# A chunked RWKV-7 / GLA encoder step: the chunk inverse in four 32x32 tiles per head pair, the decay states added by VectorE, the last chunk iteration written out

## The reference, cut to what matters

```python
def step(s, inp):                     # GLA, one chunk of 64 tokens
    ...
    o = einsum('bhts,bhsv->bhtv', scores, vc) + einsum('bhtk,bhkv->bhtv', q_e, s)
    s_new = s * exp(last)[..., None] + einsum('bhsk,bhsv->bhkv', kc * exp(last - cum), vc)

def step(s, inp):                     # RWKV-7, one token
    rt, wt, kt, vt, at, bt = inp
    sa = einsum('bhvk,bhk->bhv', s, at)
    s = s * wt[:, :, None, :] + sa[..., None] * bt[:, :, None, :] + vt[..., None] * kt[:, :, None, :]
    y = einsum('bhvk,bhk->bhv', s, rt)
...
mu = mean(y, -1); var = mean(square(y - mu), -1)          # per head of 64
y = (y - mu) * rsqrt(var + RWKV_GN_EPS) * ln_w + ln_b
y = (y + bonus) * g
out = einsum('blc,cd->bld', concatenate([o_gla, y], -1), w_out[l])
```

## Time and profile before

| | us |
|---|---|
| median of the runs | 1740.63 (1739.42 to 1741.90, three runs) |
| the profiled execution | 1739.74, its span 1737.80 |
| chunk stage and first output pair, layer 0 | 209.80 to 411.04 of the span |
| the same in layer 1 | 1060.50 to 1260.90 |

### The profile page before, as it was taken

How to read it: one execution, slowest core, us unless ns; L and a number is a source line. 1 busy time by engine, 2 the same in 40 slices (tenths; PEclk the granted TensorE clock), 3 DMA queues, 4 the chain that set the end, 5 groups by cost and what they waited for, 6 DMA issues and landing times.

```text
span 1737.8 us, 42296 instructions
## 1 busy us (share of the span) xinstructions
PE 1691.0 (97%) x19069; PEld 1634.8 (94%) x19069; DVE 905.7 (52%) x1368; ACT 665.8 (38%) x1013; POOL 570.9 (33%) x303
## 2 busy tenths in 40 slices
PE   7999999988999999999999999999799999999997
PEld 7999999968999999999999999999699999999997
DVE  4669534344566504666546873343356662166643
ACT  5444344553433212333343534544434332133323
POOL 5443301113344433344333432011133443333431
PEclk9999999999999999999999999999899999999998
DMA  5223200001222322223322221000022223222331
GB/s 146 67 68 85 80 10 4 4 3 55 86 84 81 102 75 74 86 85 95 83 74 73 74 84 46 9 4 4 7 86 85 86 80 98 66 86 86 90 94 55
DMA packets 218869, 115.51 MB, mean 66 GB/s; under 512 B 9332, under 2 KB 216450, under 8 KB 218690
## 3 DMA queue, kind: packets, MB, share of 16 engines
q1 hardware_dynamic: 218610, 112.79, 22.6%
q10 hardware_dynamic: 80, 0.02, 0.0%
HBM read 109.27 MB, written 3.53 MB: 65 GB/s over the span
## 4 chain that ended last, share of the span: by engine, by line
PE 95%; ACT 2%; DVE 1%; POOL 1%; DMA 0%; issue 0%; SPq 0%; ACTq 0%; DVEq 0%; POOLq 0%
PE ps L583 37%; PE ps L584 36%; PE ps L800 2%; PE ps L804 2%; PE ps L762 2%; PE ps L796 2%; PE ps L775 1%; PE ps L588 1%; PE ps L923 1%; PE ps L906 1%; PE ps L839 1%; PE ps L866 1%; PE ps L966 1%; PE ps L698 1%; PE ps L975 1%; PE ps L847 1%
## 5 line engine op out<-in xcount | busy, mean ns | idle before, releaser
L508 POOL TENSOR_TENSOR wlo<-raw,whi 128x1024 fp32r<-128x1024 f32 (+1 forms) x188 | 508.6, 2705 | 804.5 <-ACT whi L1120 804.4
L1120 ACT ACTIVATE whi<-raw 128x1024 fp32r<-128x1024 f32 (+1 forms) x188 | 209.5, 1114 | 651.7 <-PE ps L584 651.7
L583 PE MATMUL ps<-xh,whi 128*128 128x288 f32 x1120 | 332.8, 297 | 4.1 <-DVE xl L1498 4.1
L584 PE MATMUL ps<-xh,whi 128*128 128x288 f32 x1120 | 331.2, 296 | 0.0
L583 PE MATMUL ps<-xl,whi 128*128 128x288 f32 x1120 | 330.3, 295 | 0.0
L584 PE MATMUL ps<-xl,whi 128*128 128x288 f32 x1120 | 329.1, 294 | 0.0
L583 PE MATMUL ps<-xh,wlo 128*128 128x288 f32 x1120 | 328.9, 294 | 0.0
L584 PE MATMUL ps<-xh,wlo 128*128 128x288 f32 x1120 | 328.6, 293 | 0.0
L583 PEld LDWEIGHTS ps<-xh,whi 128*128 128x128 f32 x1120 | 210.6, 188 | 6.2 <-issue 4.5
L584 PEld LDWEIGHTS ps<-xh,whi 128*128 128x128 f32 x1120 | 210.6, 188 | 0.2
L583 PEld LDWEIGHTS ps<-xh,wlo 128*128 128x128 f32 x1120 | 210.6, 188 | 0.0
(11 more groups left out here) (278 smaller groups left out, 3314.0 us busy)
## 6 DMA issues: line engine op xcount, KB each, us to landing
raw<-in_ffn_w_up SPq DMA_DIRECT2D x88, 512.0 KB, 3.8
raw<-in_w_in SPq DMA_DIRECT2D x52, 512.0 KB, 3.7
raw<-in_ffn_w_down SPq DMA_DIRECT2D x32, 704.0 KB, 4.5
raw<-in_w_out SPq DMA_DIRECT2D x16, 512.0 KB, 3.6
xin<-in_x_prompt SPq DMA_DIRECT2D x4, 512.0 KB, 6.5
out<-xin SPq DMA_DIRECT2D x8, 256.0 KB, 2.9
out<-RW SPq DMA_DIRECT2D x16, 64.0 KB, 2.2
g<-in_rwkv_g SPq DMA_DIRECT2D x2, 256.0 KB, 2.9
```

Of the source, the lines that this page charges most:

```text
L508: e.tensor_tensor(wlo[s][:, 0:width], raw[s][:, 0:width], whi[s][:, 0:width].bitcast(F32), ALU.subtract).then_inc(w_lo[s], 1)
L583: e.matmul(acc(out)[:, 0], lhsT, rhs[:, 0:HT], start=start, stop=stop)
L584: return e.matmul(acc(out)[:, 1], lhsT, rhs[:, HT:TOK], start=start, stop=stop)
L1120: e.activation(whi[s][:, 0:width], raw[s][:, 0:width], ACT.Copy).then_inc(w_hi[s], 1)
```

## The change

**Inverse in 32x32 tiles.** `DET` and `Tf` become 32 wide: of each pair of heads the four diagonal 32x32 blocks stand under one another on the 128 partitions. A generator `blocks()` yields the four; each product of `level` is issued four times on tiles of 32 rows by 32 columns instead of twice on 64 by 64. `gram` computes the blocks of E and of its transpose by itself on tiles of 64 rows by 32 columns, `mask_inverse` is one DVE operation in place of two, and `solve_z1` and `solve_u` multiply by `Tf` in four 32x32 tiles with 64 columns moving. `copy_powers`, `add_power` and POOL's `start_inverse` handle half the columns.

**Old states on VectorE.** The products with the identity (L878, L941) are gone. `new_state` and `new_gla_state` first add the PSUM sum to `St` or `Sg`, then multiply by the decay: two DVE operations in place of one.

**Last iteration written out.** The loop now runs to i = 7. There, group 3's RWKV statistics and group 4's GLA statistics are done (tables `O_AT`, `Y_AT`), the final GLA product is DVE's (`o_last`) instead of POOL's. Behind the loop chunk 8 is solved with work put between its steps; the last group's RWKV statistics are split by chunk: chunk 7's between the solve steps, chunk 8's behind `outputs`; DVE does the bias and gate work of groups 3 and 4 that POOL did, with the gate multiplied in ahead of the statistic. Of the first output pair, 42 of 48 products of the GLA half now stand behind the last statistic and ahead of the RWKV half.

```diff
                 def level(j, X, k):
...
                     for q in range(2):
-                        for hp in range(2):
-                            h = slice(64 * hp, 64 * hp + 64)
-                            if k < 4:
-                                mm = e.matmul(powers[h, q, 0], d[h, X, q, 2], d[h, X, q, 0], start=True, stop=True)
...
+                        if k < 4:
+                            for h, b, half in blocks():
+                                mm = e.matmul(powers[b, q, 0], d[b, X, q, 2], d[b, X, q, 0], start=True, stop=True)
+                        if k < 5:
+                            for h, b, half in blocks():
+                                mm = e.matmul(powers[b, q, 1], d[b, X, q, 0], d[b, X, q, 2], start=True, stop=True)
+                        if k > 1:
+                            for h, b, half in blocks():
+                                mm = e.matmul(product[b, q], d[b, X, q, 2], d[b, X, q, 1], start=True, stop=True)
                     mm.then_inc(pe_f, 1)
...
+                def blocks():
+
+                    for c in range(4):
+                        yield slice(64 * (c // 2), 64 * (c // 2) + 64), slice(B * c, B * c + B), c % 2
...
                     for p, X, q, o in pairs(ys[:, 256:512]):
                         for h in HEADS:
                             e.matmul(o[h], tok[i % 2][h, X, 1, q, :], tok[i % 2][h, X, 2, q, :], start=True, stop=False)
-                        if i != 1:
-                            for h in HEADS:
-                                e.matmul(o[h], ident2[h, :], St[h, p, :], start=False, stop=False)
...
                 def new_state(i):
                     step(pe_b, PE_B, i, "S")
-                    e.tensor_tensor(St[:, :, :], pair3(ys[:, 256:512]),
-                                    Plast[:, :, i:i + 1].broadcast_to([P, NP, C]), ALU.mult).then_inc(dv_b, 1)
+                    new = pair3(ys[:, 256:512])
+                    if i != 1:
+                        e.tensor_tensor(St[:, :, :], St[:, :, :], new, ALU.add).then_inc(dv_b, 1)
+                        step(dv_b, DV_B, i, "Sa")
+                        new = St[:, :, :]
+                    e.tensor_tensor(St[:, :, :], new,
+                                    Plast[:, :, i:i + 1].broadcast_to([P, NP, C]), ALU.mult).then_inc(dv_b, 2 if i == 1 else 1)
...
+                solve_z(LAST)
+                back(ac_b, AC_B, LAST - 1, "Y")
+                glas(dv_g, DV_G, LAST, "Sg")
+                chunk_mean(7, gb[:, 0:256], R[:, 0:4, seventh])
+                solve_z1(LAST)
+                solve_z2(LAST)
+                solve_u(LAST)
+                ending(ac_e, AC_E, "s7")
+                chunk_mean(7, gb[:, 256:512], squares[:, :, 0:C])
+                outputs(LAST)
+                back(ac_b, AC_B, LAST, "Y")
+                pe.wait_ge(ac_o, nth(AC_O, (l + 1) * len(GROUPS) - 1, "oln"))
+                chunk_mean(8, pb[:, 0:256], R[:, 0:4, eighth])
+                out_part(0, range(0, 1))
+                ending(ac_e, AC_E, "s8")
+                chunk_mean(8, pb[:, 256:512], squares[:, :, C:2 * C])
+                back(dv_b, DV_B, LAST, "St")
+                turn_state(St, zb)
+                out_part(0, range(1, 4))
+                out_part(1, range(0, 4))
+                out_part(0, range(4, 8))
+                out_part(1, range(4, 8))
```

More of the change, by code:

```diff
@@ L32 @@
 C = 64
+B = 32
 HT = TOK // 2
@@ L199, in program @@
         tok = [cut([P, 2, 3, 2, C]) for _ in range(2)]
-        DET = [cut([P, 2, 2, 3, C]) for _ in range(2)]
-        Tf = [cut([P, NP, C]) for _ in range(2)]
+        DET = [cut([P, 2, 2, 3, B]) for _ in range(2)]
+        Tf = [cut([P, NP, B]) for _ in range(2)]
         Z, Z1, W, U = (cut([P, NP, C]) for _ in range(4))
@@ L731, in _, with turn_state @@
                         wide(PS[3], g2[:, p * P:(p + 1) * P], R[:, 13]).then_inc(pre_pe, 1)
-                def turn_state(src):
+                def turn_state(src, out):
                     for p in range(NP):
@@ L837, in solve_z1 @@
                     for p, X, q, o in pairs(zb[:, 256:512]):
-                        for h in HEADS:
-                            mm = e.matmul(o[h], Tf[i % 2][h, p, :], Z[h, p, :], start=True, stop=True)
+                        for h, b, half in blocks():
+                            mm = e.matmul(o[b], Tf[i % 2][b, p, :], Z[b, p, :], start=True, stop=True)
                     mm.then_inc(pe_b, 1)
@@ L853, in solve_u @@
                     for p, X, q, o in pairs(zb[:, 256:512]):
-                        for h in HEADS:
-                            mm = e.matmul(o[h], Tf[i % 2][h, p, :], W[h, p, :], start=True, stop=True)
+                        for h, b, half in blocks():
+                            mm = e.matmul(o[b], Tf[i % 2][b, p, :], W[b, p, :], start=True, stop=True)
                     mm.then_inc(pe_b, 1)
@@ L979, in _ @@
                 dve("ke1")
-                for i in range(-1, NCH):
+                for i in range(-1, LAST):
                     j = i + 1
-                    post = i // 2 if i >= 0 and i % 2 == 0 else None
+                    po_, py = O_AT.get(i), Y_AT.get(i)
                     if i == 0:
                         pe.wait_ge(states_loaded, (l + 1) * 64)
-                        turn_state(Sraw)
+                        turn_state(Sraw, pb)
                     if i == 1:
                         back(dv_b, DV_B, 0, "St")
-                        turn_state(St)
+                        turn_state(St, pb)
@@ L1025, in _ @@
-                    if post is not None and post > 0:
-                        post_squares_y(post - 1)
-                    if j < NCH:
-                        gla_out(j)
-                        level(j, 0, 4)
-                        level(j, 1, 4)
-                        gla_state(j)
-                        level(j, 0, 5)
-                        level(j, 1, 5)
-                last = len(GROUPS) - 1
-                def out_part(s, half):
-                    if half == 0:
+                    level(j, 0, 2)
@@ new lines, in _ @@
+                    level(j, 1, 2)
+                    gla_tokens(j)
+                    level(j, 0, 3)
+                    level(j, 1, 3)
+                    if py is not None and i < LAST - 1:
+                        post_squares_y(py)
+                    gla_out(j)
+                    level(j, 0, 4)
+                    level(j, 1, 4)
+                    if i == LAST - 1:
+                        post_squares_o(po_)
+                    gla_state(j)
+                    level(j, 0, 5)
@@ L1039, in out_part @@
+                    level(j, 1, 5)
+                def out_part(s, kts):
+                    if 0 in kts:
                         pe.wait_ge(w_lo[s], turn(s, l, PAIRS["out"]) + 1)
                         pe.wait_ge(mo_lo, (l + 1) * len(GROUPS))
-                    else:
+                    if 4 in kts:
                         pe.wait_ge(my_lo, (l + 1) * len(GROUPS))
-                    for kt in range(4 * half, 4 * half + 4):
+                    for kt in kts:
                         mm = passes(s, mh, ml, kt, KT)
-                    if half:
+                    if KT - 1 in kts:
@@ L1046, in out_part @@
                         mm.then_inc(tile_done[s], 1)
[L1048 to L1056 removed]
+                seventh, eighth = slice((LAST - 1) * C, LAST * C), slice(LAST * C, TOK)
@@ L1905, in _ @@
-                    if post is not None:
-                        scale_o(post)
-                        if post > 0:
-                            scale_y(post - 1)
-                    if i >= 1 and i % 2 == 1:
+                    for k in (2, 3, 4):
+                        add_power(j, 0, k)
+                        add_power(j, 1, k)
+                    if i == LAST - 1:
+                        mixed_o(i // 2)
+                        mixed_y(i // 2 - 1)
+                    new_gla_state(j)
@@ new lines, in _ @@
+                    add_power(j, 0, 5)
+                    add_power(j, 1, 5)
+                    if po_ is not None:
+                        scale_o(po_)
+                    if i == LAST - 1:
+                        dv.wait_ge(silu_done, (l + 1) * NP)
+                        dv.wait_ge(dv_o, (l + 1) * len(GROUPS))
+                        cc = group(po_)[1]
+                        e.tensor_tensor(G[:, 4:8, cc], G[:, 4:8, cc], G[:, 8:12, cc], ALU.mult).then_inc(o_last, 1)
+                    elif py is not None:
+                        scale_y(py)
@@ L1910, in _ @@
+                    if i >= 1 and i % 2 == 1 and i < LAST - 1:
                         mixed_o(i // 2)
```

379 lines of the change are left out of this document (209 added, 170 removed).

## The result

| | before | changed |
|---|---|---|
| median, us | 1740.9 | 1792.1 (1786.3 to 1793.4) |
| ratio | 1 | 1.029 (95% interval 1.027 to 1.031) |
| span of the profiled execution | 1737.8 | 1784.3 |
| records of PE | 19069 | 23301 |

I had forecast 1706 us, faster, with a range up to 1754. The time is outside it, and the change made the kernel slower instead of faster. The profiled execution is the fastest of the four of the changed kernel, 5.7 us under their median.

A forecast was written before the change was run, and what follows sets the result against it. PE's queue was taken as the bound, busy 97% of the span. Loop -53.6 + 36.8 + 4 = -12.8 us and endings -21.6 us sum to -34.4 us, so 1706 us; range 1668 to 1754.

The forecast's parts named there:

- Part 1: Products replaced on PE: 132.2 us removed, 78.6 us added with small records at 8.25 ns, a gain of 53.6 us.
- Part 2: Changes of tile shape on PE: 250 more at 0.147 us each cost 36.8 us, lower bound nothing.
- Part 4: Waits in the loop: PE reaches z1 earlier but ACT's copy of Z does not, 4 us back.
- Rival 1: Changing between 64x64 and smaller tiles is free, so the 36.8 us fall away: 1669 us, chance 0.14.
- Part 3: Old states by VectorE: the added DVE operations are covered by PE's work and cost nothing inside the loop.
- uncovered case: Without solve_z's 0.93 us as cover, the Sg addition delays the next gram: 0.42 us x 16, 7 us.
- Part 5: Ending from the solve of chunk 8: 25.4 us instead of 39.6; net -10.8 us per layer, 21.6 for two.
- Rival 3: Small records do not overlap: array or queue hands out one per 29.2 ns whatever its width; 1880 us, chance 0.11.
- Rival 4: Small tiles overlap only two at a time, 14.6 ns a record, 48 us more: 1754 us, chance 0.13.

The follow-up runs named there:

- e9: The changed kernel with half the products of the levels left out (3168 records of 32 columns), changes of tile shape kept: 1703.8 us.
- e4_both: The kernel before with the new ending and both old states added by VectorE, inverse left on 64x64 tiles: 1712.7 us, ratio 0.984.
- e5: The changed kernel with one 64-column product in place of two of 32 where weights are shared, 1152 records fewer: 1751.8 us, ratio 1.006 to before.
- e3: The kernel before with only the old states added by VectorE instead of by identity products: 1731.6 us, ratio 0.994.
- e1_ending: The kernel before with only the new ending (statistics regrouped, last iteration written out): 1722.4 us against 1741.4, ratio 0.989.

## Why the prediction was wrong, point by point

**The step that failed is Part 1's price of a small record, 8.25 ns.** It is the array's price and was nearly right as such: 9.4 ns in the timeline above, 8.1 in a level 1, and 0.47 us for the 48 records of a level from 306.79 to 307.26, where I had forecast 0.4. For z1 and u on four tiles with 64 columns 14.6 ns was right too (L854 at 318.61 us: its 32 records need 0.58 us with one change of shape, 14 ns each). It was used as the price in the kernel, as if instructions were always there. They come in blocks of 128 records, about one in 3.7 us when asked for as fast as possible, and the change made 6451 records of 4349 in a loop that had 29 ns to 54 ns products in nearly every block. Taking records out shows what one costs there: 27.9 ns, the lower clock included (e9). The profile before held the warning, had I divided: 151 packets for 19069 records is a block per 126 records, and 128 x 29.2 ns = 3.74 us, just at the supply's pace. The levels of before ran at the edge of it without a pause, and twice as many records in less time went over it.

The 32x32 form as a whole I had at +1.7 us (Part 1 without the identity products -39.1, Part 2 +36.8, Part 4 +4); e4_both shows it at +79.4. Of the loop's 36.8 us in layer 0, 24.7 are idle time. The other 12.1 are put down to the clock: 32 us at 0.50 at a busy share of 0.87 are worth about 14, an estimate. Without either, the loop would be near the 158.6 us that I forecast (172.1 - 14 + 2 = 160). That the pauses lower the clock is read from e4, e5 and e9, in which both shrink together, and from the pause at 216.1 us, not from a run that changes one alone.

**Part 2, changes of shape.** Right in size. In the changed kernel's timeline L784's 32 records begin 1.02 us after L776's sixteen, which need 0.87, and z2's follow 0.39 after those, which need 0.26:

```profile
385.16 1.09 PE L776 MATMUL ps<-RW 64*64 64x128 f32 x16
386.18 0.46 PE L784 MATMUL ps<-RW 64*32 64x32 f32 x32
386.57 0.68 PE L862 MATMUL ps<-work 64*64 64x64 f32 x16
```

That is 0.15 and 0.13 us against my 0.147. Rival 1 falls. The page "TensorEngine Tiling (Array Packing)" of the Trainium skill, section Tiling Modes, says that a change of mode drains TensorE; these 0.15 and 0.13 us agree with it.

**Part 3, states.** Forecast 14.5 us with cover, 7.5 without; measured 9.7. The cover failed for `Sg`, as its uncovered case said, but through z1's and `solve_z`'s waits, and not through `gram`'s. For `St` it held.

**Part 4** named the right wait (z1 for ScalarE's copy); it shows in e3 and e4 (3.8 us in all in e4, against 2.2 before). But there it comes with the addition of `Sg`, not with shorter levels; with those no run shows its size, as the pauses cover it in the changed kernel.

**Part 5, the ending.** Right in the main. 25.4 us forecast; 27.1 and 24.9 in the changed kernel, 26.8 and 25.2 in e1_ending. PE no longer waits for `ml`. It pauses 3.0 us for ScalarE and VectorE instead, and the clock did not stay at 1.00 everywhere: it was 0.89 and 0.98 in the endings of the changed kernel, 0.94 and 1.00 in those of e1. Iteration 7 became 4.9 us longer (loop of e1: 166.4), not 3.4. So 19.0 us instead of 21.6.

**Rivals.** Rival 3 was the nearest, and I gave it 0.11. Its figure of 29.2 ns a record is the supply's average, but its time, 1880, is too high by 88 us. It charged every small record, also those in blocks whose longer products make them last 3.7 us by themselves; that this makes up the difference is argued, not shown. Its picture was wrong too: the array does overlap four small tiles. The page "TensorE: Matmul & The Clock Gate" of the Trainium skill, section "Wait — 56ns, not 53.3ns?", which I cited with it, says about 25 ns from start to start at least; the levels' 9.4 ns disagree, and the measurement decides. Rival 4, 1754 us, supposed a record of 14.6 ns and is wrong in time and cause. I had put the chances on how well tiles overlap and wrote "if the queue can't deliver small records" as a last remark, without a price. It needed only one division to have one.

The page "Runtime: NRT & Kernel Launch" of the Trainium skill, section "Instruction fetch mechanics", says that the program is refilled in 16 KiB blocks of 256 instructions, which the 184 packets confirm. It also says that the fetch is hidden, because instructions are handed out more slowly than blocks fill; the 52 pauses here show a stream for which that isn't so.

## What to carry to other kernels

Before splitting products into smaller tiles, count PE's instructions per us: where 256 of them (128 float32 records) would run in under about 3.7 us, time goes by the number of instructions and no longer by columns. In such a stretch the gain lies in fewer records, wider moving sides or products that share their weights. Test a change of several parts apart: here two of three were worth 28.7 us and the third cost 79.4.

## What the runs showed of the hardware that I had not expected

- PE's program comes in 16 KB packets of 256 instructions. PE resumes 2.2 to 2.8 us after a packet starts, and the shortest distance of two packets in the changed kernel was 3.29 us. Where it ran dry, it resumed at the same place of a block, 52 times of 52.
- Four 32x32 tiles give a record each 8.1 to 9.4 ns; on 64x64 tiles a record takes 29 ns with 32 columns as with 64.
- Waits that are already satisfied cost 82 ns each between 64x64 products, half clock included, and nothing between the dense ones.
- Left open: whether the supply of blocks depends on other DMA traffic. The loops carry little (2.9% of the engines' time on q1), and I ran nothing that changes it. The longest pause of the changed kernel, 3.0 us up to 219.1, hints that it may: from 209 to 220 us q1's packets took 42.2% of the engines' time, and the packet that PE then lacked started 2.4 us after the block before had begun, against 0.7 to 1.3 us at the next ten.
